# A whole-model kernel of three blocks: another order of VectorE's steps in both attentions, and five small edits at its start, its middle and its end

## The reference, cut to what matters

```python
def reference(x, positions, ...):
    x = first_block(x, positions, norm_mix, w_in, ..., norm_final)       # block 1
    return second_block(x, norm_mix_pre_2, ..., ffn_w_down_2)            # blocks 2 and 3

    # the attention of block 3, per 128 queries:
    logits = jnp.einsum('bqhd,bkhd->bhqk', qi, k) + (ci[..., :, None] - c[..., None, :])
    p = jax.nn.softmax(jnp.where(mask, logits, -jnp.inf), axis=-1)
    o = jnp.einsum('bhqk,bkhd->bqhd', p, v)

    # each of its sublayers ends with a norm of the branch's output, the last one too:
    x = x + rmsnorm_2(y, norm_ffn_post[layer])
```

## Time and profile before

| | us |
|---|---|
| three runs | 2144.57, 2145.3, 2139.97; median 2144.57 |
| the profiled execution, its own time | 2142.03 |
| its span in the profile | 2140.2 |
| TensorE busy | 2066.3 (97% of the span) |
| VectorE busy | 1220.8 (57%) |
| ScalarE busy | 795.5 (37%) |
| GpSimd busy | 21.3 (1%) |
| chain that ended last | TensorE 88%, VectorE 5%, ScalarE 2%, issue 1%, a DMA 1% |
| mean granted TensorE clock | 0.987 |

### The profile page before, as it was taken

How to read it: one execution, slowest core, us unless ns; L and a number is a source line. 1 busy time by engine, 2 the same in 40 slices (tenths; PEclk the granted TensorE clock), 3 DMA queues, 4 the chain that set the end, 5 groups by cost and what they waited for, 6 DMA issues and landing times.

```text
span 2140.2 us, 25567 instructions
## 1 busy us (share of the span) xinstructions
PE 2066.3 (97%) x9936; PEld 1674.0 (78%) x9944; DVE 1220.8 (57%) x1719; ACT 795.5 (37%) x1236; POOL 21.3 (1%) x45
## 2 busy tenths in 40 slices
PE   7899999999999999999999999999999999999996
PEld 6776778888888888877788888878786678888885
DVE  5669645455444355456575564663537757647375
ACT  4239243232212133245343342442427734323242
POOL 1000000000000000000000000000000000000000
PEclk9989999999999999999999999999999999999998
DMA  4410412222222222321122223222220022222221
GB/s 168 158 60 1 128 50 93 104 99 99 99 98 99 99 98 77 120 89 59 60 98 98 98 79 113 70 94 89 99 99 21 21 79 79 98 98 98 99 83 54
DMA packets 34240, 188.52 MB, mean 88 GB/s; under 512 B 4440, under 2 KB 8696, under 8 KB 14400
## 3 DMA queue, kind: packets, MB, share of 16 engines
q1 hardware_dynamic: 31296, 179.41, 23.8%
q0 software_dynamic: 1696, 5.72, 1.0%
q10 hardware_dynamic: 1152, 2.10, 0.3%
HBM read 182.54 MB, written 2.11 MB: 86 GB/s over the span
## 4 chain that ended last, share of the span: by engine, by line
PE 88%; DVE 5%; ACT 2%; issue 1%; DVEq 1%; PEld 1%; DMA 1%; PEldq 0%; POOL 0%; SPq 0%; ACTq 0%; POOLq 0%
PE bank L409 23%; PE bank L411 23%; PE bank L410 23%; PE bank L486 4%; PE bank L491 4%; PE bank L487 4%; PE bank L1196 2%; PE bank L1166 1%; PE bank L645 1%; DVE w_lo L357 1%; PE bank L2205 1%; PE bank L1183 1%; ACT w_hi L343 1%; PE bank L2197 1%; DVEq L1238 0%
## 5 line engine op out<-in xcount | busy, mean ns | idle before, releaser
L343 ACT ACTIVATE w_hi<-w_raw 128x2048 fp32r<-128x2048 f32 (+3 forms) x174 | 314.4, 1807 | 812.0 <-PE bank L411 689.6
L409 PE MATMUL bank<-a_hi,w_hi 128*128 128x512 f32 x1376 | 540.3, 393 | 3.7 <-DVE shared L2546 1.6
L411 PE MATMUL bank<-a_hi,w_lo 128*128 128x512 f32 x1376 | 536.5, 390 | 0.0
L410 PE MATMUL bank<-a_lo,w_hi 128*128 128x512 f32 x1376 | 536.5, 390 | 0.0
L357 DVE TENSOR_TENSOR w_lo<-w_raw,w_hi 128x2048 fp32r<-128x2048 f32 (+3 forms) x174 | 374.8, 2156 | 143.7 <-ACT w_hi L343 143.5
L409 PEld LDWEIGHTS bank<-a_hi,w_hi 128*128 128x128 f32 x1376 | 258.9, 188 | 60.0 <-issue 3.4
L411 PEld LDWEIGHTS bank<-a_hi,w_lo 128*128 128x128 f32 x1376 | 258.8, 188 | 54.2
L410 PEld LDWEIGHTS bank<-a_lo,w_hi 128*128 128x128 f32 x1376 | 259.0, 188 | 53.3 <-issue 0.2
L409 PE MATMUL bank<-big_halves,w_hi 128*128 128x512 f32 x616 | 240.6, 391 | 3.1 <-DVE w_lo L357 3.0
L411 PE MATMUL bank<-big_halves,w_lo 128*128 128x512 f32 x616 | 239.8, 389 | 0.0
L410 PE MATMUL bank<-big_halves,w_hi 128*128 128x512 f32 x616 | 239.7, 389 | 0.0
(11 more groups left out here) (340 smaller groups left out, 2432.6 us busy)
## 6 DMA issues: line engine op xcount, KB each, us to landing
w_raw<-in_w_fu SPq DMA_DIRECT2D x44, 1024.0 KB, 4.8
w_raw<-in_w_up SPq DMA_DIRECT2D x16, 1024.0 KB, 4.8
w_raw<-in_w_down SPq DMA_DIRECT2D x16, 1024.0 KB, 4.8
w_raw<-in_w_fd SPq DMA_DIRECT2D x16, 1024.0 KB, 4.8
w_raw<-in_w_fd SPq DMA_DIRECT2D x8, 768.0 KB, 4.3
w_raw<-in_w_rqk SPq DMA_DIRECT2D x4, 1024.0 KB, 5.0
w_raw<-in_w_rvg SPq DMA_DIRECT2D x4, 1024.0 KB, 5.0
w_raw<-in_w_gate SPq DMA_DIRECT2D x4, 1024.0 KB, 4.8
```

What stands on the lines that cost most here:

```text
L343: act.activation(w_hi[slot][:, cols], raw[slot][:, cols], ACT.Copy).then_inc(hi_half_ready.sem if half == 0 else hi_ready.sem, 1)
L409: pe.matmul(out, w[0], x[0], start=first, stop=False)
L410: pe.matmul(out, w[0], x[1], start=False, stop=False)
L411: return pe.matmul(out, w[1], x[0], start=False, stop=last)
```

## The change

1. **The start.** ScalarE's queue loads only tile 0 of `xT`; SyncE's loads the first half of the first weights, tile 1, the second half, then tiles 2 to 7. The first block is split in halves: ScalarE makes half of `w_hi` after tile 0's `a_hi` and half after tile 1's, VectorE does so with `w_lo`, and TensorE waits for the first half ahead of the first tile and for the second ahead of the fifth. ScalarE runs one small activation before the first load has landed, so that its table load stands ahead of that wait.
2. **First keys' partners.** The four DMAs of n = 0 are issued from ScalarE's queue, those of the queries from GpSimd's as soon as the stage "q" is done, and the memset of `blk` stands ahead of the last four DMAs.
3. **Both attentions.** VectorE's `take` comes one step later, and `stage_low` behind `weigh` and `take`. The values are read in place, without the eight copies of `stage_values`. The small exponential that makes ScalarE load its table ahead of the attention now stands in `begin_act`, for both attentions (before, only block 3 had it).
4. **The last update.** GpSimd adds tiles 1, 3 and 5, VectorE the other five.
5. **Addresses.** `mean_of` is declared ahead of `ident_b`, and the three columns of 16 bytes behind `warm`: the buffers from `ident_b` to `gains` now begin at multiples of 64 bytes.

```diff
         def update_and_store(src, vec, root):
+            b_sc, b_pool = scaled.n, pool_step.n
+            lent = (1, 3, 5)
+            own = [k for k in range(KT) if k not in lent]
+            def scale(dve, k):
+                if k >= 4 and k - 4 in lent:
+                    dve.wait_ge(pool_step.sem, b_pool + lent.index(k - 4) + 1)
...
+                dve.scalar_tensor_tensor(work4[:, k % 4, :], src[:, k, :], gain(vec, k), bank[6][:, :],
+                                         ALU.mult, ALU.mult).then_inc(scaled.sem, 1)
             def vector(dve):
                 root[1](dve, lambda: None)
                 for k in range(KT):
-                    scale_tile(dve, src, vec, k, b_sc, b_up)
-                    if k >= 1:
-                        add_tile(dve, k - 1, b_sc)
-                add_tile(dve, KT - 1, b_sc)
+                    scale(dve, k)
+                    if k >= 1 and k - 1 in own:
+                        add(dve, k - 1, updated)
+                add(dve, KT - 1, updated)
+            def gpsimd(pool):
+                for k in lent:
+                    add(pool, k, pool_step)
...
         def first_tiles():
             def sync(sp):
                 sp.dma_start(gains[:, :], io["gains"]).then_inc(gains_in.sem, 16)
-                load(sp, specs["q"], 0, 0, 0)
+                sp.dma_start(raw[0][:, 0:n], specs["q"].packed[0, :, 0:n]).then_inc(first_half_in.sem, 16)
+                tile(1)
+                sp.dma_start(raw[0][:, n:], specs["q"].packed[0, :, n:]).then_inc(raw_loaded[0].sem, 16)
+                for k in range(2, KT):
+                    tile(k)
...
             def ahead_act(act, second_block):
-                for k in range(KT):
-                    act.dma_start(xT[:, k, :], io["x_tiles"][:, k, :]).then_inc(x_in[k].sem, 16)
+                act.dma_start(xT[:, 0, :], io["x_tiles"][:, 0, :]).then_inc(x_in[0].sem, 16)
+                act.wait_ge(pool_step.sem, b_pool + 3)
+                act.activation(warm[:, :], warm[:, :], ACT.Copy)
...
-                    if k == 0:
-                        act.wait_ge(raw_loaded[0].sem, 16)
-                        act.activation(w_hi[0][:, :], raw[0][:, :], ACT.Copy).then_inc(hi_ready.sem, 1)
+                    if k < 2:
+                        act.wait_ge((first_half_in, raw_loaded[0])[k].sem, 16)
+                        cols = columns_of(SLOT, k)
+                        act.activation(w_hi[0][:, cols], raw[0][:, cols], ACT.Copy).then_inc((hi_half_ready, hi_ready)[k].sem, 1)
...
         def attention(...):
-                    vals = v_of(n) if static else v_st[p]
+                    vals = v_of(n)
...
                 def step(s, unit):
                     if unit(0) is not None:
                         maximum(unit(0))
-                        if s % U == 0 and s // U + 1 < pairs:
-                            stage_low(dve, s // U + 1)
                     if unit(1) is not None:
                         weigh(unit(1))
-                    if last_of(unit(5)):
-                        take(unit(5))
-                steps(6, step)
+                    if last_of(unit(6)):
+                        take(unit(6))
+                    if s % U == 0 and unit(0) is not None and s // U + 1 < pairs:
+                        stage_low(dve, s // U + 1)
+                steps(7, step)
...
                 stage_high(act, 0)
+                act.activation(warm[:, :], one[:, :], ACT.Exp)
...
-                        if not static and s % U == 0:
-                            stage_values(s // U)
...
             def swaps(pool):
                 pool.wait_ge(pool_step.sem, b_pool + 3)
-                pool.wait_ge(evacuated.sem, e_q + 3)
-                partners(pool, 0, k_swapped[:, 0:1, :], qk[:, 4:5, :])
+                pool.wait_ge(evacuated.sem, e_q + 2)
                 partners(pool, 1, q_swapped[:, :, :], qk[:, 0:4, :])
+                pool.wait_ge(tables_act.sem, 3)
+                pool.memset(blk[:, :, :, :, NC:CB], 0.0).then_inc(pool_step.sem, 1)
                 pool.wait_ge(evacuated.sem, e_q + 4)
                 partners(pool, 2, k_swapped[:, 1:3, :], qk[:, 6:8, :])
-                pool.memset(blk[:, :, :, :, NC:CB], 0.0).then_inc(pool_step.sem, 1)
+            def first_swap(act, b, slot, m):
+                if b == 0:
+                    act.wait_ge(pool_step.sem, b_pool + 3)
+                    act.wait_ge(evacuated.sem, e_q + 3)
+                    partners(act, 0, k_swapped[:, 0:1, :], qk[:, 4:5, :])
```

More of the change, by code:

```diff
@@ L239, in build @@
         ret_ssq, ret_root = (sb(top, n, [P, RH, TT]) for n in ("ret_ssq", "ret_root"))
+        one = sb(top, "one", [P, 1])
         def big_tiles(i, first=0, tiles=KT, dt=F32):
@@ L452, in dense @@
         def dense(name, chunks, early_dve=none, late_dve=none, early_act=none, late_act=none, tile_ready=None,
[L453 removed]
+                  ahead_dve=next_weights, ahead_act=next_weights, with_tile=None, between=None, lag=None, halved=False):
             spec, nxt, m = specs[name], after(name), marks()
@@ L470, in tensor, with begin @@
             def tensor(pe):
-                def begin(b, q):
-                    pe.wait_ge(lo_ready.sem, m["lo"] + b + 1)
+                def begin(b, q, half=False):
+                    if half:
+                        pe.wait_ge(lo_half_ready.sem, 1)
+                    else:
+                        pe.wait_ge(lo_ready.sem, m["lo"] + b + 1)
                     pe.wait_ge(evacuated.sem, m["evac"] + b - 1)
@@ L497, in by_tile @@
                 def by_tile():
-                    first = begin(0, 0)
+                    first = begin(0, 0, halved)
                     tiles = len(first[1][0])
                     for k in range(tiles + (lag or 0)):
+                        if halved and k == tiles // 2:
+                            pe.wait_ge(lo_ready.sem, m["lo"] + 1)
                         if k < tiles:
@@ L928, in update_and_store, with add @@
         def update_and_store(src, vec, root):
-            b_sc, b_up = scaled.n, updated.n
+            b_sc, b_pool = scaled.n, pool_step.n
+            lent = (1, 3, 5)
+            own = [k for k in range(KT) if k not in lent]
+            b_up = updated.n
+            def scale(dve, k):
+                if k >= 4 and k - 4 in lent:
+                    dve.wait_ge(pool_step.sem, b_pool + lent.index(k - 4) + 1)
+                elif k >= 4:
+                    dve.wait_ge(updated.sem, b_up + own.index(k - 4) + 1)
+                dve.scalar_tensor_tensor(work4[:, k % 4, :], src[:, k, :], gain(vec, k), bank[6][:, :],
+                                         ALU.mult, ALU.mult).then_inc(scaled.sem, 1)
+            def add(eng, k, done):
+                eng.wait_ge(scaled.sem, b_sc + k + 1)
+                eng.tensor_tensor(xT[:, k, :], xT[:, k, :], work4[:, k % 4, :], ALU.add).then_inc(done.sem, 1)
             def vector(dve):
@@ L944, in update_and_store @@
             scaled.n += KT
-            updated.n += KT
-            return {"vector": vector, "scalar": root[0], "sync": sync}
+            updated.n += len(own)
+            pool_step.n += len(lent)
+            return {"vector": vector, "scalar": root[0], "sync": sync, "gpsimd": gpsimd}
         def first_tiles():
@@ L1018, in first_tiles @@
             return {"sync": sync, "gpsimd": gpsimd}, dict(ahead_act=ahead_act, ahead_dve=ahead_dve, tile_ready=halves_ready(b_hi, b_lo),
-                                                          between={(0, "end"): end_of_first, (1, 2): in_second})
+                                                          between={(0, "end"): end_of_first, (1, 2): in_second}, halved=True)
         def scaled_to(dst, scale=1.0):
@@ L1118, in attention @@
             units = U * pairs
-            v_st = [x[:, :].rearrange("p (j d) -> p j d", d=P) for x in (total, inv)]
             probs_t = [lent[0:2], lent[2:4]]
@@ L1575, in kcvc_late @@
                     blocks(dve)
-            stages.append(dense("kcvc", two_chunks(a_tiles), scaled_to(qk[:, 4:8, :]), kcvc_late,
+            stages.append(dense("kcvc", two_chunks(a_tiles), scaled_to(qk[:, 4:8, :]), kcvc_late, none, first_swap,
                                 between={(0, 8): positions_turned, (1, 12): halves_swapped}))
@@ L2701, in fox @@
                     lambda dve: split_low(dve, range(KT - 1)))
-                def begin_exp(act):
-                    begin_act(act)
-                    act.activation(warm[:, :], warm[:, :], ACT.Exp)
                 def begins(begin):
                     return lambda eng, b, slot, m: begin(eng) if b == 2 else None
-                stages.append(dense("fq", two_chunks(a_tiles), scaled_to(qT, float(FD) ** -0.5), begins(begin_dve), none, begins(begin_exp)))
+                stages.append(dense("fq", two_chunks(a_tiles), scaled_to(qT, float(FD) ** -0.5), begins(begin_dve), none, begins(begin_act)))
                 stages += [attend, {"scalar": split_high, "vector": lambda dve: split_low(dve, [KT - 1])}]
```

42 lines of the change are left out of this document (23 added, 19 removed).

## The result

| | before | after |
|---|---|---|
| median beside each other | 2141.49 us (5 runs) | 2128.15 us (5 runs, 2125.32 to 2130.40) |
| ratio of the times | | 0.993, 95% interval 0.9919 to 0.994 |
| profiled execution / its span | 2142.03 / 2140.2 | 2125.32 / 2123.5 |

The kernel is 0.7% faster. 2127.5 us was forecast, within 2121 to 2135. The total came out, several of its terms did not. The table shows where. A landmark is one instruction of TensorE, and a row gives the us at which TensorE reaches it in both traces. The difference is the lead of the changed kernel.

What follows compares the result with a forecast made beforehand. TensorE, busy 97% of the span, was taken as the bound, so only its waits and both ends could be won. Terms 4.0 + 2.1 + 2.0 + 3.3 + 2.8 + 2.0 = 16.2 us gave 2125.8 to 2128.4, taken as 2127.5, range 2121 to 2135.

Steps and rivals of the forecast that it cites:

- Start, 4.0: Before the first matmul: reordered, halved first loads let TensorE start at 8.0 instead of 12.0, 4.0 us; bounds 2.5 to 4.3.
- Partners, 2.1: Rotated first key tile: issued from ScalarE's queue, its partners land earlier, TensorE goes on 2.1 us earlier; bounds 0.7 and 2.9.
- Blocks, 2.0: Blocks' memset ahead of GpSimd's four DMAs: TensorE's waits of 1.54 and 0.46 us go, 2.0 us, at least 1.5.
- Block 3, 3.3: Block 3's attention: five pairs of heads fall from 9.75 to 9.13 us, plus the opening, 3.3 us; bounds 1.5 and 4.5.
- the two edits are worth something together: Block 3's pairs: moving VectorE's output lets ScalarE's exponential start 0.64 us earlier only since the copy of values goes too.
- Block 1, 2.8: Block 1's attention: moved output 1.2 us, opening with early table load 1.6 us, together 2.8; bounds 1.3 and 4.3.
- with the gap down to 0.6 I expect the same here: Block 1's opening: with TensorE's gap at 0.6 us the clock keeps 2.4 GHz, as in block 3's opening.
- Last update, 2.0: Behind the last matmul: VectorE gives 3 of 8 additions to GpSimd, at 1.1 us each there; 2.0 us, bounds 0.5 and 2.1.
- Addresses, 0: Buffers moved to multiples of 64 bytes: worth nothing.
- Rival 3: Everything comes, and the clock's part in block 1's opening in full, 4.3 instead of 1.6 us: 2124.8 us; chance 0.07.
- Rival 2: The flow of loads binds the start and the rotated keys, 1.5 and 1.5 us less gain: 2130.5 us; chance 0.12.
- rivals 1 and 4: 1: attentions don't get shorter, 2132, chance 0.14; 4: "ISA" code load delays GpSimd's end additions, 2130.8 or 2151.5, chance 0.05.

Runs made afterwards that it cites:

- same again: The changed kernel once more with no edit, in another execution: 2130.91 us against 2125.32 us for the profiled one.
- memset late: The changed kernel with the memset of the blocks behind the last four partners on GpSimd's queue again: 2132.50 us, one execution.

## Why the prediction held, point by point

**Start, 4.0.** Right at the first matmul, too large as a term: 2.4 to 2.6 are left ahead of the rotated key in the two executions, 3.2 to 3.4 in the run that undoes it. The step that failed is the one from 4.0 at the first matmul to 4.0 in the sum. The text's own figures had the second block's `w_lo` 2.2 earlier, wanted 4.0 earlier, with 0.9 of room, which leaves a stall of 0.9; "no new stall above 1 us" put it at nothing. In the profile after, `w_lo` ended 1.3 us earlier (ScalarE had stood for the second half) and TensorE stood 0.8, 0.9 of lead. In same again the half landed 0.6 earlier and there is no stall, but TensorE ran at 1.2 GHz for 4.6 us behind its first matmul instead of 3.0, which took 0.7. In both, the wait ahead of the second block of "kcvc" grew from 0.65 to 1.1 (1.08 in the profile after), another 0.4.

**Partners, 2.1.** Wrong: 0.1. From the taking out of the key tile to the landing of its partners it took 8.39 us, for a forecast 6.3 and 8.43 before. Half of the miss is the issues: ScalarE's took 0.63 to 1.24 each, not 0.5, and the fourth stood at 50.49, 1.1 late. The other half is the landing: the step "I take 4.7, as the queries' partners no longer run beside it" named the wrong neighbour; it took 5.72, held by the 4 MB that SP's queue issues in the same microseconds (1.97 without them). The bound of 0.7 was too high. On top, the clock fell behind this wait and took 1.7 us, in same again 2.7. Whether it falls there differs from execution to execution: behind waits of 3.2 to 4.1 us it fell in eight executions and stayed in three, the kernel before among them, and it never fell there in the three without a wait.

**Blocks, 2.0.** Mechanism right, size 2.6 to 2.7 (memset late): the whole 2.6 us for which VectorE waited comes back, not only what TensorE's list names.

**Block 3, 3.3.** 3.0: five pairs of 9.75 become 9.16; the opening gives nothing where 0.2 was expected. But "the two edits are worth something together" is wrong. The earlier trace rows already held the refutation: ScalarE stood 0.75 us for the maximum with the copy in place, more than the 0.62 to be won.

**Block 1, 2.8.** 3.35 in the profile, 2.6 in same again. The pairs gave 1.3 for 1.2, the table 1.36 for a forecast 1.30. The step "with the gap down to 0.6 I expect the same here", a clock that stays up, failed: it dropped in this opening in ten of the twelve executions with an early table load, and held in this profile, which has a gap of 0.85, and in one other. The Trainium skill (ScalarE: Activation LUTs, What ACT_TABLE_LOAD costs) has 2.66 us for the switch; the run with the late table shows about 1.4 on TensorE's path, so the page's drain is not seen here.

**Last update, 2.0.** 2.54, above the upper bound of 2.1. The term missed the ring: with two buffers each scaling waited for the addition just ahead of it, 0.72 us after its start instead of 0.60, which the timeline of before shows and the text read as plain issue ("0.70 each with the start of the next"). GpSimd's addition was 1.64 for a forecast 1.1 and hid all the same. The Trainium skill (SBUF — State Buffer, Who interferes with whom) has additions on the two engines exclude each other; the trace agrees in part: GpSimd's took 1.26 alone and 1.64 when it started 0.17 behind one of VectorE's, which is 0.38 longer where 0.51 of VectorE's was still to run, and VectorE's paid only where it started second.

**Addresses, 0.** Right.

**Sum.** Taken without the clock as far as it can be, the terms are 2.6 + 0.1 + 2.6 + 3.0 + 2.6 + 2.5 = 13.4 us, the medians' difference is 13.3; some 0.5 between the two attentions belongs to no term, in both executions. Forecast were 16.2; the choice of 2127.5 instead of 2125.8 took 1.7 of the excess back. That the number came within 0.7 us is thus in part luck. So is the profiled 2125.32 beside 2125.8: clock that was not forecast (3.2 us at 107 alone) stood in for the partners. Rival 3's 2124.8 is as near to that one execution, but not all came. Rival 2 (the flow binds the start and the keys, 2130.5) had the cause right for the keys; rivals 1 and 4 did not come: the pairs are shorter, and GpSimd's first addition began 0.09 us behind its scaling, so whatever the row "ISA" stands for was not on the path.

## What to carry to other kernels

A small transfer that waits on the critical path is to be asked what else is issued in its microseconds; moving it to another queue won nothing, holding back two large loads by 4 to 5 us won 4 and kept the clock from falling behind the wait. Before crediting a removed instruction, look whether its engine was waiting there anyway: an idle time longer than the gain says that it was not the bound. And a saving of a few us is to be read at landmarks inside the trace, in two executions, as one execution's clock can give or take as much as the edit.

## What was not expected of the hardware

- Two executions of one kernel differ by 5.5 us: in the first 200 us three falls of TensorE's clock to 1.2 GHz against one short one, at the same instructions and behind nearly the same wait (3.3 us).
- The clock can fall where TensorE shows no idle time: in same again it fell at 105.2, and TensorE was busy 7.00 of the 7.00 us from 98 to 105. The last 3 us of them are 64 small products, which stand ahead of the fall at 107.3 in the profile before too; in the profile after the same 64 stand at 100.92 and nothing falls. Why stays open.
```profile
102.14 4.27 PE L1495 MATMUL bank<-shared,big 64*128 64x32 f32 x64
```
- ScalarE's queue took 0.63 to 1.24 us to issue a DMA of 16 KB where GpSimd's took 0.52 to 0.67.
- At the start ScalarE's table load waited for nothing and ended at 2.49, though an instruction that waits for a memset stands behind it; 4.8 had been forecast.
- GpSimd's addition of 128x512: 1.26 us alone, 1.64 beside VectorE's.
